# Token halves in four norms, context halves first in a feed-forward stage: a 17-stage fp32 transformer kernel

## What is computed

```python
def _modulate(t, g, shift, scale):
    return _rms(t, g) * (1 + scale) + shift
def _swiglu(h, w13, w2):
    gte, up = jnp.split(h @ w13, 2, axis=-1)
    return (jax.nn.silu(gte) * up) @ w2
...
x = rms_norm(x + gate * y, final_g)
for i in range(2):
    mod, modc = (silu(c) @ mod_w[i] + mod_b[i]), (silu(c_ctx) @ mod_w[i] + mod_b[i])
    lat = lat + 0.5 * mod[0, 2] * _swiglu(_modulate(lat, ...), ffn_w13[i, 0], ffn_w2[i, 0])
    cx  = cx  + 0.5 * modc[0, 2] * _swiglu(_modulate(cx, ...), ffn_w13[i, 0], ffn_w2[i, 0])
    h, hc = _modulate(lat, ...), _modulate(cx, ...)
    y, yc = conv_mixer(h, hc) if i == 0 else attention(h, hc)
    lat = lat + mod[1, 2] * y
    lat = lat + 0.5 * mod[2, 2] * _swiglu(_modulate(lat, ...), ffn_w13[i, 1], ffn_w2[i, 1])
    ...
```

## Time and profile before

| | us |
|---|---|
| median of 3 runs | 2079.53 (2076.51 to 2079.58) |
| the profiled execution | 2075.76 |
| its span, first to last instruction | 2073.9 |
| PE busy | 1906.5 (92% of the span) |
| DVE busy | 1397.0 (67%) |
| ACT busy | 689.9 (33%) |
| POOL busy | 128.0 (6%) |

### The profile page before, as it was taken

How to read it: one execution, slowest core, us unless ns; L and a number is a source line. 1 busy time by engine, 2 the same in 40 slices (tenths; PEclk the granted TensorE clock), 3 DMA queues, 4 the chain that set the end, 5 groups by cost and what they waited for, 6 DMA issues and landing times.

```text
span 2073.9 us, 26722 instructions
## 1 busy us (share of the span) xinstructions
PE 1906.5 (92%) x10092; PEld 1621.9 (78%) x10092; DVE 1397.0 (67%) x2081; ACT 689.9 (33%) x926; POOL 128.0 (6%) x78
## 2 busy tenths in 40 slices
PE   2986799799999998998999999999999998879998
PEld 2955788688888877876888888778888887669998
DVE  7878899876666666668666666676665226755554
ACT  2454355422222223332222222232222213444432
POOL 2001200200000110003000001100000010010000
PEclk9987899799999999998999999999999999999999
DMA  9843854423443452334333444433343233223444
GB/s 378 319 169 78 227 199 176 174 105 138 152 152 133 157 187 112 136 138 171 118 131 146 152 144 155 178 114 132 148 152 108 96 110 113 83 82 142 168 160 158
DMA packets 75738, 315.79 MB, mean 152 GB/s; under 512 B 19060, under 2 KB 22904, under 8 KB 56344
## 3 DMA queue, kind: packets, MB, share of 16 engines
q1 hardware_dynamic: 75136, 314.15, 42.7%
q10 hardware_dynamic: 536, 0.79, 0.1%
HBM read 313.86 MB, written 1.06 MB: 152 GB/s over the span
## 4 chain that ended last, share of the span: by engine, by line
PE 74%; DVE 18%; ACT 3%; issue 2%; DMA 1%; POOL 1%; SPq 0%; DVEq 0%; ACTq 0%
PE acc L1318 72%; DVE Wl L832 4%; ACT Wh L527 2%; DVE tmp L819 2%; PE psN L1318 1%; DVE psGT L861 1%; DVE psGT L867 1%; DVE psGT L864 1%; DVE najunk L867 1%; DVE najunk L864 1%; DVE small L989 1%; DVE XT L819 1%; DMA afirst<-in_ada_w 1%; PE psN L1380 1%; DVE tmp L1007 1%
## 5 line engine op out<-in xcount | busy, mean ns | idle before, releaser
L1318 PE MATMUL acc<-Hh,Wh 128*128 128x512 f32 (+1 forms) x2320 | 808.4, 348 | 48.7 <-DVE Hl L819 23.3
L1318 PE MATMUL acc<-Hl,Wh 128*128 128x512 f32 (+1 forms) x2320 | 799.5, 345 | 0.0
L1318 PE MATMUL acc<-Hh,Wl 128*128 128x512 f32 (+1 forms) x2320 | 798.9, 344 | 0.0
L832 DVE TENSOR_TENSOR Wl<-raw,Wh 128x2048 fp32r<-128x2048 f32 (+1 forms) x214 | 449.6, 2101 | 270.3 <-ACT Wh L527 270.2
L1318 PEld LDWEIGHTS acc<-Hh,Wh 128*128 128x128 f32 x2320 | 447.9, 193 | 112.9 <-issue 46.7
L527 ACT ACTIVATE Wh<-raw 128x2048 fp32r<-128x2048 f32 (+1 forms) x214 | 374.3, 1749 | 343.0 <-PE acc L1318 329.6
L1318 PEld LDWEIGHTS acc<-Hl,Wh 128*128 128x128 f32 x2320 | 448.5, 193 | 50.4 <-issue 0.7
L1318 PEld LDWEIGHTS acc<-Hh,Wl 128*128 128x128 f32 x2320 | 447.4, 193 | 50.5
L1318 PE MATMUL acc<-hidh,Wh 128*128 128x512 f32 (+1 forms) x704 | 258.6, 367 | 0.9 <-DVE Wl L832 0.9
L1318 PE MATMUL acc<-hidl,Wh 128*128 128x512 f32 (+1 forms) x704 | 258.3, 367 | 0.0
L1318 PE MATMUL acc<-hidh,Wl 128*128 128x512 f32 (+1 forms) x704 | 258.2, 367 | 0.0
(11 more groups left out here) (222 smaller groups left out, 1187.7 us busy)
## 6 DMA issues: line engine op xcount, KB each, us to landing
raw<-in_ffn_up SPq DMA_DIRECT2D x88, 1024.0 KB, 4.8
graw<-in_mod_w SPq DMA_DIRECT2D x144, 512.0 KB, 5.5
raw<-in_ffn_down SPq DMA_DIRECT2D x64, 704.0 KB, 4.1
graw<-in_ada_w SPq DMA_DIRECT2D x32, 512.0 KB, 5.7
raw<-in_odd_in SPq DMA_DIRECT2D x16, 1024.0 KB, 4.9
raw<-in_even_in SPq DMA_DIRECT2D x12, 1024.0 KB, 7.0
raw<-in_conv_in SPq DMA_DIRECT2D x12, 1024.0 KB, 4.8
afirst<-in_ada_w SPq DMA_DIRECT2D x8, 1024.0 KB, 13.0
```

The source lines that it names most:

```text
L832: nc.vector.tensor_tensor(Wl[:, half, 0:f], raw[:, slot, 0:f], Wh[:, half, 0:f].bitcast(f32), ALU.subtract)\
L1318: return nc.tensor.matmul(out, lhsT, rhs, start=start, stop=stop)
```

## The change

1. **Norms of `conv_in`, `ffn1_up`, `ffn2_up`, `gqa_kv` by token halves.** The last tile of the stage before (in down stages the last pair, tiles 14 and 15) is computed for the latent tokens first and for the context tokens after them. The residual, squares, sums, mean, power and spread of the latent half are put beside the context half's products. The next stage's tiles 0 and 1 are then taken as four parts of 256 columns: tile 0 latent (chunk by chunk, with the context's sums behind chunk 3 and its spread behind chunk 7), tile 1 latent, tile 0 context, tile 1 context. The weight splits that ran before the first chunk (tile 1; behind down stages the split of tile 0 too) are cut into halves of 1024 columns and put between the chunks.
2. **`ffn0_up` begins with its context half.** The context's factor is spread into the free right half of bank `psT[1]` during `odd_out`. Context chunks are scaled and multiplied first; the sums of the latent tokens (24 small products, which stood alone) stand between chunks 3 and 4 of tile 0, the spread between chunks 3 and 4 of tile 1. The eight `final_g` operations move from the norm's end to the end of `ffn0_up`.
3. **A split later:** in `ffn0_up`, `ffn1_up` and `ffn2_up` the split of tile 2 stands in step 0 behind the tanh (ACT) and the second product (DVE).
4. **Dots moved:** `conv_out` goes from two pairs of dots per tile to one, `gqa_out` from none to one; four pairs move, their number stays.
5. Steps that stood in loops are written out where halves need it; PE's program grows from 4,165 to 5,424 rows.

The diff, cut to its core:

```diff
@@ STAGES
-    ("conv_out", 4, 16, 0, TOK, 2, "dve"),
+    ("conv_out", 4, 16, 0, TOK, 1, "dve"),
...
-    ("gqa_out", 4, 16, 0, LAT, 0, "dve"),
+    ("gqa_out", 4, 16, 0, LAT, 1, "dve"),
...
+        HALVED = {n: i for i, n in enumerate(["conv_in", "ffn1_up", "ffn2_up", "gqa_kv"])}
+        LAST = {n: (KC - 2, KC - 1) if n == "ffn1_up" else (KC - 1,) for n in HALVED}
+        PAIRED = ("ffn0_up", "ffn1_up", "ffn2_up")
@@ DVE
+            def halves_norm(name, meanwhile):
...
+                dve.wait_ge(lat_done, l + 1)
+                residual_half(0, CL).then_inc(lat_res, 1)
+                meanwhile()
+                mean(0, psN, lat_ss, l + 1).then_inc(lat_mean, 1)
+                if not ffn:
+                    split(S[name].n0)
+                dve.wait_ge(lat_spread, l + 1)
+                scaled(0, 0, CL, psN).then_inc(lat_t, 1)
+                for k in range(KC):
+                    if k + 1 < KC:
+                        if k > 0:
+                            dve.wait_ge(lat_ready, KC * l + k)
+                        scaled(k + 1, 0, CL, psN).then_inc(lat_t, 1)
+                    if ffn and k < 2:
+                        split_half(S[name].n0, k)
+                    dve.wait_ge(lat_hi, KC * l + k + 1)
+                    low(k, 0, CL).then_inc(lat_ready, 1)
+                    if k in (5, 7):
+                        split_half(S[name].n0 + 1, k // 2 - 2)
+                    if k == 2:
+                        dve.wait_ge(tile_done, s.n0 + s.tiles)
+                        residual_half(1, CC).then_inc(drained["dve"], 1)
+                    if k == 5:
+                        mean(1, psT[1], n_ss, i + 1).then_inc(n_mean, 1)
+                dve.wait_ge(n_spread, i + 1)
...
@@ PE
+            def first_two_halved(s):
...
+                pe.wait_ge(lo_ready, s.n0 + 1)
+                part(0, CL, lat_ready, KC * l, {3: ctx_sums, 7: ctx_spread})
+                pe.wait_ge(lo_ready, s.n0 + 2)
+                pe.wait_ge(drained["dve"], prev.drained1)
+                part(1, CL, lat_ready, KC * l, {})
+                part(0, CC, h_ready, H0[name], {}).then_inc(tile_done, 1)
+                part(1, CC, h_ready, H0[name], {}).then_inc(tile_done, 1)
...
+                def last_halved():
...
+                    part(0, 0, CL)
+                    sum_of_sums(name)
+                    part(0, 1, CL).then_inc(lat_done, 1)
+                    part(1, 0, CC, lat_sums).then_inc(tile_done, 1)
+                    lat_spreads(name)
+                    part(1, 1, CC).then_inc(tile_done, 1)
...
-            norm("ffn0_up")
-            linear(S["ffn0_up"])
+            part(0, CC, ctx_ready, 0, range(4))
+            sum_of_sums("ffn0_up")
...
+            part(0, CC, ctx_ready, 0, range(4, KC))
+            part(1, CC, ctx_ready, 0, range(4))
...
+            part(1, CC, ctx_ready, 0, range(4, KC))
+            part(0, CL, h_ready, H0["ffn0_up"], range(KC)).then_inc(tile_done, 1)
+            part(1, CL, h_ready, H0["ffn0_up"], range(KC)).then_inc(tile_done, 1)
```

More of the change, by code:

```diff
@@ L212, in build @@
         c_tanh = sem("c_tanh")
+        ctx_spread0, ctx_t, ctx_hi, ctx_ready = (sem("ctx_" + x) for x in ("spread0", "t", "hi", "ready"))
+        hi_half = sem("hi_half")
+        lat_done, lat_res, lat_sq, lat_ss, lat_mean, lat_rstd, lat_spread, lat_t, lat_hi, lat_ready = (
+            sem("lat_" + x) for x in ("done", "res", "sq", "ss", "mean", "rstd", "spread", "t", "hi", "ready"))
         nmx = small[:, 0:64]
@@ L595, in step @@
                         .then_inc(ffn_th, 1)
+                    if s.name in PAIRED and isinstance(t, int) and t == 0:
+                        split(s.n0 + 2)
                     act.wait_ge(ffn_hf, s.ffn0 + t + 1)
@@ L962, in step @@
                 def step(t, u, i):
+                    if halved(s) and isinstance(t, int) and t == s.tiles - 1:
+                        modulation_of(s, t, u, i)
+                        return
                     next_split(s, t, u, i)
@@ L1344, in step @@
                     last.then_inc(tile_done, 1)
-                if begin:
-                    for t in range(begin, s.tiles):
+                if begin or halved(s):
+                    for t in range(begin, min(s.tiles, 4)):
                         step(t, t % SPLIT, t // SPLIT)
+                    if s.tiles > 4:
+                        tiles(pe, s, SPLIT, 0, lambda t, u, i: None if isinstance(t, int) and t < 4 else step(t, u, i), head=2)
+                elif s.name in HALVED:
+                    first_two_halved(s)
+                    tiles(pe, s, SPLIT, 0, lambda t, u, i: None if isinstance(t, int) and t < SPLIT else step(t, u, i), head=1)
                 else:
@@ L1546, in _, with part @@
             last.then_inc(tile_done, 1)
+            pe.wait_ge(n_pow, 1)
+            for b in range(QB):
+                ins = spread(psT[1][:, LAT + b * P:LAT + (b + 1) * P], rctx, b)
+            ins.then_inc(ctx_spread0, 1)
             linear(S["odd_out"], begin=1)
-            norm("ffn0_up")
-            linear(S["ffn0_up"])
+            s, i = S["ffn0_up"], NORMS["ffn0_up"]
+            def part(t, c, ready, base, chunks):
+                for k in chunks:
+                    pe.wait_ge(ready, base + k + 1)
+                    for j in range(2):
+                        last = three(acc[t][j][:, c], (s.n0 + t) % SPLIT, j * KC + k, Hh[:, k, c], Hl[:, k, c], k == 0, k == KC - 1)
+                return last
@@ L1550, in _, with keys @@
+            linear(S["ffn0_up"], begin=SPLIT)
             ffn_down(S["ffn0_down"])
-            norm("conv_in")
             linear(S["conv_in"])
             linear(S["conv_out"], xh=cyh, xl=cyl)
-            norm("ffn1_up")
             linear(S["ffn1_up"])
             ffn_down(S["ffn1_down"])
-            norm("ffn2_up")
             linear(S["ffn2_up"])
             ffn_down(S["ffn2_down"])
-            norm("gqa_kv")
             s, n0 = S["gqa_kv"], S["gqa_kv"].n0
             d0 = s.drained0
+            def keys(c, ready, base):
+                for k in range(KC):
+                    pe.wait_ge(ready, base + k + 1)
+                    for j in range(2):
+                        last = three(acc[0][j][:, c], n0 % SPLIT, j * KC + k, Hh[:, k, c], Hl[:, k, c], k == 0, k == KC - 1)
+                    if c == CL and k == 3:
+                        ctx_sums("gqa_kv")
+                    if c == CL and k == 7:
+                        ctx_spread("gqa_kv")
+                return last
```

276 lines of the change are left out of this document (245 added, 31 removed).

## The result

The changed kernel takes 2061.68 us (median of 4 runs, 2061.17 to 2062.41), against 2078.02 (2076.19 to 2079.58, 4 runs) for the kernel before: ratio 0.9922, 95% interval 0.9905 to 0.9939, 16.3 us less. The forecast was 2065, with a range of 2060 to 2073. The profiled execution took 2061.41 us; its span is 2059.6 where it was 2073.9, so 14.3 us less, against a sum of 14.5.

The account below looks back on a forecast made before the run. PE was taken as the bound, with time to win only where it waits or runs slowly. Terms of 15.8 us less 1.3 gave 14.5, so 2075.8 became 2061.3; the median, 3.8 above, was 2065, range 2060 to 2073.

Parts of the forecast that it names:

- What bounds it: Whole kernel: PE, at work for 92% of the span, is the bound; time can be won only where it waits or runs slowly.
- The halved norm: Worked at conv_in: latent part from 778.2, both context parts ending at 805.4 instead of 808.5, a gain of 3.2 us.
- ffn1_up: Norm before ffn1_up: fewer dots put DVE on time, two tiles end at 997.1 against 1003.0; gain 5.9 us, bounds 3.2 and 6.8.
- The second rival: Latent parts of the halved norms: PE starts into a slow clock, costing some 7.5 us for four, 2072; chance 0.13.
- gqa_out: Dots moved here make residuals late and delay ffn3_up's norm: a loss of 3.8 us, bounds 2.8 and 5.9.
- ffn0_up: Context first gains 3.8 us, final_g operations before ffn0_down lose 0.8; net 2.8, bounds 2 and 3.8.
- The split of tile 2: In three up stages: a later split costs nothing if it ends before tile 1 does; uncovered, up to 2.3 us each.
- Split products: Linear and down-stage products of 512 columns become two of 256 at 0.120 us each: 7.5 us in all, already inside the walks.
- The sum: Whole kernel: terms add to 15.8 us, less 1.3 is 14.5, giving 2061.3 for an execution like the profiled one; median 2065.
- ffn2_up: Halved norm before ffn2_up: the same walk as for conv_in gives a gain of 3.3 us.
- gqa_kv: Halved norm before gqa_kv: value groups between the key's halves give longer cover; gain 4.4 us, bounds 3.2 and 4.8.
- added waits: Whole kernel: some thirty added waits between engines that are in no walk, 0.03 to 0.05 us each, cost 1.3 us.

## Why the prediction was right

**What bounds it** was read rightly: PE's busy time stayed, and its idle and slow time at the borders gave the gain.

**The halved norm** was right in mechanism and nearly in size. The walk of conv_in had PE starting the latent part at 778.2 and ending its last product at 805.4; on the same axis (the changed execution runs 0.9 ahead there) it was 778.2 and 804.7. The gain was 3.9 for 3.2; the half splits fell where the walk had them (DVE 774.02, 776.08, 782.55, 785.20). All four halved norms together were worth 13.8 us, by the run without halves.

**ffn1_up** was mis-sized: 4.2 for 5.9. The step that failed is "The latent half is then ready as PE ends the stage." At conv_in it is, since 33 products of the context half, 4.0 us, stand behind the spread (772.67) and cover "scaled", `Hh` and "low" of the first chunks. At ffn1_up no product stands behind the spread: it comes at 962.47, at the stage's end, and PE then waits 1.73 us for the first chunk. That DVE's split of tile 0 is started 0.1 us before POOL's power, which then takes 2.69 for 0.71 us, I missed as well, but it makes only 0.3 of the spread's time. And behind the gaps the clock falls (970.1 to 976.9): with the gaps filled 1.7 came back. The rule of the Trainium skill that I weighed for the dots ("SBUF — State Buffer", Who interferes with whom) would have told me of the long power as well.

**The second rival**, a slow clock in the latent part, came true in one of the four norms, at ffn1_up and behind its gaps. At the others PE's gaps are about 0.40, 0.66 and 1.01 each time, and the clock was 1.00.

**gqa_out** was right in mechanism: the last residual is 3.4 us late for a forecast of 3.8. Of this only 2.3 reach ffn3_up's tiles, less than my lower bound of 2.8, since its chunks then meet a clock that rises sooner. What the Trainium skill's rule on shared access ("SBUF — State Buffer", Who interferes with whom) gave, 2.8 to 3.3, was nearer than my 3.8.

**ffn0_up** was 3.6 and 1.1 for 3.8 and 0.8. (3.8 less 0.8 is 3.0; the prediction has 2.8, 0.2 too little in its sum.) The sentence that only the latent pass is left was too kind to the kernel: in front of it PE still waits 10.10 us, 6.6 of them for DVE's dots in odd_out (the gap is 3.53 without them). I counted these as given, because the change doesn't touch them; they were part of the largest single wait left.

**The split of tile 2** I took for a later one and costed at nothing while its cover holds. It stands earlier than before (0.5 us behind the start of the first tanh on ACT for 3.5), and the part is needed: without it the new order has 4.8 us of waits and is 5.2 slower by the median.

**Attention** had no term. It took 1.2 us more, and has one stretch at the low clock that the kernel before doesn't have.

**Split products**: a product of 256 columns took 0.120 us (in conv_in's second tile six begin every 0.72 us), as the rows had it. The formula for an isolated product in the Trainium skill ("TensorE: Matmul & The Clock Gate", Back-to-back issue gap) would give an estimate of 0.109 for 256 columns; the page says itself that it counts too little for small products between weight loads, and the trace agrees with that.

**The sum** was met to 0.1 us for the profiled execution (2061.3 forecast, 2061.41 measured), and that is in part luck. ffn1_up gave 1.7 less than its term, the attention took 1.2 and the way up to odd_out, with the same work in both kernels, 1.6, both without a term. Against that stand conv_in, ffn2_up and gqa_kv with 0.7, 0.6 and 0.3 more, gqa_out with 1.5 less lost, and 1.3 for added waits that did not show. The median is 3.3 below the forecast because I took it to lie 3.8 above the profiled execution, as in the three runs before; here it lies 0.3 above.

## What to carry to other kernels

Cutting the last tile of a stage and the first of the next by tokens hides a norm that needs the whole row, but only if what the norm needs (adds, residual, splits) is not queued behind optional work. Put such work (here products for later use) into stages whose tiles are long against the helper engine's work, not into the short ones at a border: that was worth nearly as much here as the change itself (14.2 us against 16.3 by the medians). Look also at what stands behind the spread in the tensor engine's program: where nothing did, a wait of 1.7 us stayed. And after an order is tightened, look again at every operation that shares a port with another engine's critical step.
